# A scatter-add of whole rows of expert outputs, cut into two halves of 512 columns

## The reference

```python
D_MODEL = 1024; SEQ = 1024; N_EXPERTS = 16; TOP_K = 2; D_EXPERT = 256

def hier_moe(h, router_wg, router_bg, router_we, router_be, exp_w1, exp_w3, exp_w2):
    ...
    gate = jnp.sum(jax.nn.one_hot(expert_id, N_EXPERTS, dtype=jnp.float32) * top_w[..., None], axis=1)
    y = jnp.zeros((B * S, D), jnp.float32)
    for e in range(N_EXPERTS):
        hid = jax.nn.silu(xt @ exp_w1[e]) * (xt @ exp_w3[e])
        y = y + gate[:, e:e + 1] * (hid @ exp_w2[e]).astype(jnp.float32)
    return y.reshape(B, S, D).astype(h.dtype)

def trunk(x, ...):
    h = layer_norm(x, ln_in_g, ln_in_b)
    for l in range(DEPTH):
        mix = mixer(h, ...)          # attention and a gated linear recurrence, side by side
        h = layer_norm(DEEPNORM_ALPHA * h + mix, ln1_g[l], ln1_b[l])
        ffn = hier_moe(h, ...)
        h = layer_norm(DEEPNORM_ALPHA * h + ffn, ln2_g[l], ln2_b[l])
    return h
```

## Time and profile before

| | us |
|---|---|
| median of 3 runs | 1660.35 |
| lowest and highest of them | 1652.62, 1660.93 |
| the profiled execution | 1657.61 |
| its span (first to last instruction) | 1655.9 |
| its mean granted TensorE clock | 0.943 |

### The profile page before, as it was taken

One profiled execution on the slowest core, in us unless ns is written; L12 is line 12 of the kernel. 1 busy time (PEld: TensorE's weight loads), 2 busy tenths in 40 slices (PEclk: granted clock), 3 DMA queues, 4 the chain that ended last, 5 costly groups with the idle time before them and its releaser, 6 DMA issues. The chain is left out here.

```text
span 1655.9 us, 29919 instructions
## 1 busy us (share of the span) xinstructions
PE 1490.1 (90%) x9130; PEld 1307.0 (79%) x9131; DVE 1102.4 (67%) x2101; ACT 904.5 (55%) x1527; POOL 490.9 (30%) x345
## 2 busy tenths in 40 slices
PE   5999989999897999999999999985699999999940
PEld 5999967787687899999999999981577788777830
DVE  8788539999834877788877778877543433444237
ACT  3444447878734655655565566632465544555325
POOL 1221125665510011111112111121445444554318
PEclk9999999999956999999999999996899999999975
DMA  8865443444243212211111212116699777796566
GB/s 280 313 220 210 176 154 126 154 166 178 108 137 124 69 34 96 65 69 57 58 59 57 95 60 74 46 53 215 193 267 273 197 220 192 209 274 174 108 206 263
DMA packets 124005, 249.58 MB, mean 151 GB/s; under 512 B 22290, under 2 KB 75538, under 8 KB 123924
## 3 DMA queue, kind: packets, MB, share of 16 engines
q1 hardware_dynamic: 93984, 160.97, 28.0%
q0 software_dynamic: 12528, 45.62, 11.8%
q10 hardware_dynamic: 17412, 41.96, 6.6%
HBM read 153.98 MB, written 94.54 MB: 150 GB/s over the span
## 5 line engine op out<-in xcount | busy, mean ns | idle before, releaser
L1690 DVE TENSOR_TENSOR d_probs_t_lo<-d_pt_ps,d_probs_t_hi 128x512 fp32r<-128x512 f32 x256 | 164.6, 684 | 70.4 <-ACT d_probs_t_hi L1615 69.2
L1854 POOL TENSOR_TENSOR d_h_tile<-d_s_tile,d_ln_g_b 128x512 f32<-128x512 f32 x30 | 38.9, 1297 | 554.7 <-ACT d_s_tile L1636 536.1
L1615 ACT ACTIVATE d_probs_t_hi<-d_pt_ps 128x512 fp32r<-128x512 f32 x256 | 139.2, 595 | 110.3 <-PE d_pt_ps L1494 103.9
L1666 DVE TENSOR_REDUCE d_neg_max<-d_s_ps 128x1 f32<-128x1024 f32 x128 | 155.5, 1215 | 3.3 <-PE d_s_ps L1483 3.3
L121 PE MATMUL acc<-k_hi,wl_hi 128*128 128x256 f32 x512 | 144.6, 283 | 4.5 <-DVE k_lo L577 4.5
L1598 ACT ACTIVATE d_probs<-d_s_ps,d_neg_max 128x1024 f32<-128x1024 f32 x128 | 143.4, 1120 | 4.3 <-DVE d_neg_max L1666 4.3
L121 PE MATMUL e_a_ps<-up_hi,e_xt_hi 128*128 x336 | 137.1, 408 | 8.7 <-issue 4.4
L122 PE MATMUL acc<-k_lo,wl_hi 128*128 128x256 f32 x512 | 143.7, 281 | 0.0
L123 PE MATMUL acc<-k_hi,wl_lo 128*128 128x256 f32 x512 | 143.6, 280 | 0.0
L1512 PE MATMUL d_ot_ps<-d_probs_t_hi,d_v_split 128*128 128x256 f32 x512 | 127.5, 287 | 10.0 <-DVE d_probs_t_lo L1690 10.0
L1494 PE MATMUL d_pt_ps<-ident,d_probs 128*128 128x128 f32 x1024 | 133.7, 274 | 2.8 <-ACT d_probs L1598 2.8
(11 more groups left out here) (404 smaller groups left out, 4106.8 us busy)
## 6 DMA issues: line engine op xcount, KB each, us to landing
up_raw<-in_exp_w SPq DMA_DIRECT2D x32, 1024.0 KB, 10.3
down_raw<-in_exp_w SPq DMA_DIRECT2D x16, 1024.0 KB, 11.7
d_h_tile<-h_dram SPq DMA_DIRECT2D x16, 522.0 KB, 4.8
h_dram<-v_all ACTq DMA_DIRECT2D x16, 512.0 KB
ht_hi_dram<-k_hi ACTq DMA_DIRECT2D x8, 1024.0 KB, 4.3
ht_lo_dram<-k_lo ACTq DMA_DIRECT2D x8, 1024.0 KB, 6.7
q_dram<-wq_raw ACTq DMA_DIRECT2D x16, 512.0 KB, 2.9
d_q_tile<-q_dram SPq DMA_DIRECT2D x16, 512.0 KB, 3.9
```

The source lines that it names most:

```text
L1615: act.activation(pt_hi[:, c * HALF:(c + 1) * HALF, h % 2], pt_ps[c][:], ACT.Copy).then_inc(pth_done[c], 1)
L1666: dve.tensor_reduce(nm[:, u, h:h + 1], s_ps[h % 2][:], AX, ALU.max, negate=True).then_inc(nm_done, 1)
L1690: dve.tensor_tensor(pt_lo[:, part, h % 2], pt_ps[c][:], pt_hi[:, part, h % 2].bitcast(F32), ALU.subtract)\
```

## The change

The sums lie in two tensors of 512 columns each, `sum_dram[0]` and `sum_dram[1]`, instead of one of 1024. Each tile's scatter becomes two, one per half of the columns, each to its own tensor and with its own semaphore `y_added[c]`. The scatter of half c waits for ScalarE's half c of the tile and for the scatter of half c of the tile before. All stores and loads of the sums are cut in two in the same way, and the counts that are waited for follow.

```diff
-    sum_dram = nc.dram_tensor("sum_dram", (T + P, D), F32, kind="Internal").ap()
+    sum_dram = [nc.dram_tensor(f"sum_dram{c}", (T + P, D // 2), F32, kind="Internal").ap() for c in range(2)]
...
             def store_h1(t):
                 sp.wait_ge(h1_done, 2 * t + 2)
-                for dst in (h1_dram, sum_dram):
-                    sp.dma_start(dst[bass.ds(t * P, P), :], h1[:]).then_inc(h1_stored, 16)
-
-            sp.sem_inc(h1_stored, 32)
+                sp.dma_start(h1_dram[bass.ds(t * P, P), :], h1[:]).then_inc(h1_stored, 16)
+                for c in range(2):
+                    sp.dma_start(sum_dram[c][bass.ds(t * P, P), :], h1[:, c * 512:(c + 1) * 512]).then_inc(h1_stored, 16)
+
+            sp.sem_inc(h1_stored, 48)
...
             sp.wait_ge(last_h1, 2)
-            for dst in (h1_dram, sum_dram):
-                sp.dma_start(dst[T - P:T, :], s_t[1][:, 0:D]).then_inc(h1_stored, 16)
-            sp.wait_ge(h1_stored, 32 * NT + 64)
+            sp.dma_start(h1_dram[T - P:T, :], s_t[1][:, 0:D]).then_inc(h1_stored, 16)
+            for c in range(2):
+                sp.dma_start(sum_dram[c][T - P:T, :], s_t[1][:, c * 512:(c + 1) * 512]).then_inc(h1_stored, 16)
+            sp.wait_ge(h1_stored, 48 * NT + 96)
...
             last = sp.value_load(last_tile[0:1, 0:1], min_val=1, max_val=MT - 1)
-            sp.wait_ge(y_added, 16 * last + 16)
-            sp.nop(nofuse=True)
-            for t in range(EARLY):
-                sp.dma_start(first_rows[t], sum_dram[t * P:(t + 1) * P, :]).then_inc(rows_in[t], 16)
+            for c in range(2):
+                sp.wait_ge(y_added[c], 16 * last + 16)
+                sp.nop(nofuse=True)
+                for t in range(EARLY):
+                    sp.dma_start(first_rows[t][:, c * 512:(c + 1) * 512], sum_dram[c][t * P:(t + 1) * P, :]).then_inc(rows_in[t], 16)
...
             def down(j, u):
                 pool.wait_ge(gate_done, j + 1)
                 pool.nop(nofuse=True)
-                pool.wait_ge(yt_done[0], j + 2)
-                pool.nop(nofuse=True)
-                pool.wait_ge(yt_done[1], j + 2)
-                pool.nop(nofuse=True)
-                need(pool, y_added, 16 * j)
-                pool.nop(nofuse=True)
-                pool.indirect_dma_start(sum_dram, bass.IndirectOffsetOnAxis(sx[u][:, 0:1], 0), yt[u][:], None,
-                                        compute_op=ALU.add).then_inc(y_added, 16)
+                for c in range(2):
+                    pool.wait_ge(yt_done[c], j + 2)
+                    pool.nop(nofuse=True)
+                    need(pool, y_added[c], 16 * j)
+                    pool.nop(nofuse=True)
+                    pool.indirect_dma_start(sum_dram[c], bass.IndirectOffsetOnAxis(sx[u][:, 0:1], 0),
+                                            yt[u][:, c * 512:(c + 1) * 512], None, compute_op=ALU.add).then_inc(y_added[c], 16)
...
-                need(dve, y_added, 16 * (j - 1))
-                dve.nop(nofuse=True)
+                for c in range(2):
+                    need(dve, y_added[c], 16 * (j - 1))
+                    dve.nop(nofuse=True)
...
             for t in range(EARLY, NT):
-                sp.dma_start(x[t], sum_dram[t * P:(t + 1) * P, :]).then_inc(x_in[t], 16)
+                for c in range(2):
+                    sp.dma_start(x[t][:, c * 512:(c + 1) * 512], sum_dram[c][t * P:(t + 1) * P, :]).then_inc(x_in[t], 16)
```

More of the change, by code:

```diff
@@ L2215, in experts @@
         gate_done = sem("gate_ready")
-        y_added = sem("y_added")
+        y_added = [sem(f"y_added{c}") for c in range(2)]
         block = ctx.enter_context(nc.Block())
@@ L2348, in _ @@
             last = run_tiles(pool, skip, ahead, None, skip, skip, down, skip, split_rest)
-            pool.wait_ge(y_added, 16 * last + 16)
-            pool.nop(nofuse=True)
+            for c in range(2):
+                pool.wait_ge(y_added[c], 16 * last + 16)
+                pool.nop(nofuse=True)
             pool.wait_ge(x_in[1], 8 * last + 24)
```

10 lines of the change are left out of this document (5 added, 5 removed).

## The result

The changed kernel is slower: 1668.95 us (median of 6 runs, 1661.28 to 1676.55) against 1655.51 us (6 runs of the kernel before, 1651.55 to 1660.93). The ratio on record is 1.0069, 95% interval 1.004 to 1.0098, so 11.4 us (6.6 to 16.2); the quotient of the two medians, 1.0081 or 13.4 us, lies within that interval. The forecast was +0.2 us, and its range was 1652 to 1669 us. The profiled execution of the changed kernel took 1676.55 us with a span of 1674.8 us; it is the slowest of its six, so its trace shows the loss enlarged.

A forecast was written before the change was run, and what follows sets the result against it. TensorE's matmuls bound the expert stage, the scatter only the tail. Terms 0 + 0 + 0 + 0.2 = +0.2 us gave 1657.8 us against the profiled 1657.6, 1660.5 on the median's scale; range 1652 to 1669 us.

The forecast's parts named there:

- TensorE as busy as now: Sign of being right: in the expert loop, from 1200 to 1500 us, TensorE's busy share stays unchanged.
- its three signs of being wrong: TensorE's first matmul waiting for up_lo; DMA share near full in the loop; last stage's first load sooner with the stage.
- Part 1, GpSimd's order: Expert loop: second scatter makes GpSimd 1.89 us later, within up_lo's slack of 2.36 us at the tightest; price zero.
- Part 1, the last sentence: Expert loop: VectorE's added wait ahead of the gate copy is for a scatter already landed; zero.
- Part 2, the DMA engines: Expert loop: 2 KB packets and 1.0 us more start per tile raise DMA share to 88%; zero on TensorE.
- Part 3, the tail: After the last matmul: landing seen 0.9 us sooner, given back by SyncE's twelve issues; zero, -1.7 to +3.8 us.
- The third rival: Tail: the last landing, not SyncE's issues, sets the barrier; 0.9 us gained, up to 2.6; chance 12%.
- The halves don't land apart: Tail: the queue runs both halves as one, so SyncE's twelve issues start later; +2.8 us, 1663.3 us; chance 10%.
- Part 4, the last stage: Final layer norm: twenty loads behind the barrier, no engine waits for one; zero, bound 1.4 us.
- Part 5: Attention stage: one more store per tile, the last issued 0.4 us later; +0.2 us (0 to +0.5).
- The loop breaks: Expert loop: GpSimd's delay stalls TensorE at two-tile experts, from 3 us on; 15 us at 5 us, 1675 us; chance 8%.

The follow-up runs named there:

- the moved gate copy: VectorE's gate copy put behind the next tile's hidden rows: 0.9974 in the changed kernel, 0.9976 in the kernel before, both against the kernel before.
- ScalarE's loads above: Changed kernel with gate copy moved and weights signalled early, ScalarE instead of SyncE issuing the six early loads of half 1: 0.9947 to the kernel before.
- The runs with doses: Kernel before, whole scatters, a memset behind each making GpSimd 1.0, 3.5 or 4.8 us later: 1.0008, 1.0136 and 1.0206.
- the kernel with both repairs: Gate copy moved behind the hidden rows and weights signalled early: 0.9940 in the changed kernel, 0.9955 in the kernel before, both against the kernel before.
- the kernel with halved loads: Kernel before with one tensor and one scatter per tile, but stores and loads of the sums cut in two: 1.0024.
- the kernel with the memset of 1400 columns: Kernel before, one scatter per tile, with a GpSimd memset of 1400 columns behind each scatter that nothing waits for just then: 1.0008.
- the kernel with the small memset: Kernel before, one scatter per tile, with a GpSimd memset of 250 columns behind each scatter, awaited before going on: 1.0136.

## Where the prediction was right and where it was wrong, point by point

The measured median of 1668.95 us lies within the stated range, 0.05 us below its upper end. That is luck and no credit to the mechanism: the forecast was +0.2 us, the loss was 11.4, and the upper part of the range was there for a TensorE that waits for `up_lo`, which it didn't. Of its own signs of being right, "TensorE as busy as now" failed, with 94.2 us of 100 against 97.5; none of its three signs of being wrong clearly appeared. It looked for the loss on the wrong way.

**Part 1, GpSimd's order: the amount right, the price of zero wrong.** The issue of a half was put at 1.59 us and measures 1.58, the delay at 1.89 us and `up_lo` comes 2.1 to 2.2 us later. (The lower bound of 0.4 us leaves out one gap; two issues of 0.98 us with two gaps of 0.30 against 1.89 are 0.67 us. Nothing rests on it.) And, as forecast, TensorE never waits for up_lo on GpSimd. The step that failed is the list of those who wait for what is behind the scatter. It named TensorE as the only waiter for `up_lo` and `down_lo`, and measured the slack on that way alone: 3.09 us, 2.36 at the tightest. SyncE waits for the same `down_lo`, and its signal to ScalarE stands behind that wait. The trace of before has ScalarE waiting for the signal already, 11.9 us in 4 waits, so what makes `down_lo` later could make `up_hi` later. The runs put the price of this way at 3.6 us of the profiled loop.

**Part 1, the last sentence: "it is for the scatter of two tiles back, which has landed: zero".** This is the dearer error: the moved gate copy gives the changed kernel 1% of its time and the kernel before 0.24%, and the traces show 6.6 us in the four tiles and 4.7 us of lost clock behind three of them. The list of waits of the kernel before has this very wait, 3 times with 1.3 us in all, so it had not always landed. What moved it further: lateness adds up on GpSimd over a tile, from the two scatters over the weights and the gather to the next tile's second half, which started 3.3 us later than the whole one had; and VectorE has to see the later half landed. The half's shorter way makes up for 1.6 us of that: in the tail a whole scatter is seen landed 6.30 us after its start, a half after 1615.51 - 1610.77 = 4.74 us.

**Part 2, the DMA engines: right.** The 0.52 MB of scatter and as much of gather per tile took 45.6% x 360/38.66 = 4.25 us of DMA time per MB, and take 46.6% x 360/37.17 = 4.51, so some 0.3 us more per tile where 1.0 us was allowed for. The packets of 2 KB cost next to nothing. By the figures of the Trainium skill ("DMA: Bandwidth & Descriptors", section "Anatomy of one DMA"), 2.0 us plus the bytes at 436 GB/s, a half was, as an estimate, to land 0.6 us sooner than a whole. The trace disagrees: 6.30 - 4.74 = 1.56 us sooner in the tail (5.98 to 6.30 us in the seven profiles with whole scatters, 4.48 to 4.84 in the seven with halves), and the measurement decides. The transfer of 3.6 us that I read from the earlier trace rows for 0.52 MB, and the 2.3 us for half of it, fit that: 1.3 us.

**Part 3, the tail: the steps right, the end wrong by 1.3 us.** Against the end of ScalarE's last output (1589.15 before, 1609.34 after) the half scatters were to go out at 1.75 and 3.65 us, and went at 1.43 and 3.46; SyncE was to start at 6.55 us and end its twelve issues at 12.15, and did so at 6.17 and 12.20 (12.18 before). So the issues did give the landing back. But "the end of SyncE's issues opens the last stage" didn't hold for the kernel before: its barrier opened 14.66 us after the last output, 2.48 us behind the issues, and now it opens at 13.32, 1.12 us behind them. The third rival ("the barrier is set by the last landing") had the mechanism of before; its gain was 1.3 us, between the 0.9 and the 2.6 that it names, and the issues then took over as the limit. "The halves don't land apart" is refuted by SyncE's start 2.1 us ahead of half 1's earliest landing (1612.80 + 4.85 = 1617.65, with the 4.85 us from ScalarE's loads above).

**Part 4, the last stage: the price right.** From VectorE's first instruction behind the barrier to the end it takes 52.1 us before (1655.9 - 1603.81) and after (1674.8 - 1622.66). VectorE does wait 1.9 us for its first half tile, which the forecast had excluded; the stage's end doesn't show it.

**Part 5: not told apart.** The first expert tile starts anywhere from 1164.65 to 1173.40 us in the 14 profiles, with a mean of 1168.8 for two stores per tile and 1169.2 for three. 0.2 us can't be seen in that; nor do the 2.35 us of the first two profiles mean anything.

**The rivals.** "The loop breaks" was the right family, at 8%: GpSimd is late and TensorE stalls. But it decided from a delay of 3 us, because it had the same single waiter in view as part 1. The runs with doses put the knee near 1 us, and the slope at 8.5 to 9 us for each further us of lateness, that is 0.9 x 8.5 = 8 us for the 1.9 us that the forecast itself had, as an estimate from that line.

## What to carry to other kernels

Before an engine is made later for nothing, search the list of waits of the kernel before for every wait, on any engine, that ends with something it makes or something queued behind it: a wait of some tenths of a microsecond there, three times in 42, says that its waiter has no slack left, whatever the slack on the way that you had in view. It doesn't say what the lateness costs: here 1.0 us of it made the waits more (the gate copy's from 1.3 to 2.7 us, ScalarE's for the signal from 11.9 to 20.1 us) and the kernel 1.3 us longer, which can't be told from nothing, and the change's 2.1 us cost 11.4. A wait ahead of a tiny bookkeeping copy holds everything behind it on VectorE; put the copy behind the work that the critical engine needs, and give signals before waits that don't concern them. Once both were done here, the split cost nothing in the loop (396.5 and 396.6 us), and the kernel with both repairs is the best measured, with the split or without it: 0.994 (0.9916 to 0.9963) and 0.9955 (0.9939 to 0.9971), whose difference can't be told from nothing.

## What the runs showed of the hardware

**A short idle can cost TensorE half its clock for three more microseconds.** Behind the idle of the first chain's tile (12, the one behind tile 11), TensorE of the changed kernel (stretches of 1 us, columns as in the earlier trace rows):

```profile
1298.00:1299.00 1.00, 0.00 (x0) 0.00 (x0) 0.85 (x5) 0.04 (x1) 0.00 (x0) 1.00 0.00 0
1299.00:1300.00 1.00, 0.33 (x1) 0.34 (x2) 0.00 (x0) 0.96 (x1) 0.77 (x1) 0.90 0.00 0
1300.00:1301.00 1.00, 1.00 (x3) 0.73 (x3) 0.52 (x1) 1.00 (x2) 0.70 (x2) 0.50 0.21 25
1301.00:1302.00 1.00, 1.00 (x4) 0.79 (x3) 0.71 (x1) 0.04 (x1) 1.00 (x1) 0.50 0.56 143
1302.00:1303.00 1.00, 1.00 (x4) 0.81 (x3) 0.00 (x0) 0.00 (x0) 1.00 (x1) 0.50 0.86 352
```

The granted clock is 0.50, the level of 1.2 GHz, for three microseconds of full work after some two without a matmul, and the tile takes 11.07 us where its like take 9.5. In the kernel before, a place with almost as much idle (three slices busy for 0.32, 0.44 and 0.70) kept 1.00:

```profile
1416.00:1417.00 1.00, 0.32 (x2) 0.00 (x0) 1.00 (x3) 0.86 (x2) 0.00 (x0) 1.00 0.00 0
1417.00:1418.00 1.00, 0.44 (x2) 0.20 (x2) 1.00 (x3) 0.43 (x2) 0.00 (x0) 1.00 0.00 0
1418.00:1419.00 1.00, 0.70 (x3) 0.62 (x4) 0.76 (x5) 0.03 (x1) 0.00 (x0) 1.00 0.00 0
```

In the changed kernel's profile four tiles of 42 are lengthened so, by 1.5 to 2.6 us, 7 us of the 17.8 together; the kernel before has none. One of the four is the second tile of the stage, behind a stall that the kernel before has too; the other three, 4.7 us, stand behind waits of the first chain. In the kernel with halved loads the place that kept 1.00 above had 1.62 us of idle in three slices and not 1.54; there the clock fell to 0.50 and the tile behind took 11.06 us. So a stall of some 2 us cost 1.5 to 2.6 us more than itself, and not each time: the second tile of the stage is hit in 5 of the 9 profiles in which the first one has stalled TensorE.

**GpSimd's rows overlap.** What comes behind a scatter whose row is 1.6 us long starts while that row still lasts, mostly 1.0 to 1.2 us after it began (1.15 in the earlier trace rows, 1.02 in the kernel with the memset of 1400 columns), unless it is another scatter, which starts 1.88 us after it. And in the kernel with the small memset, the wait for it kept GpSimd idle for more than three times its length:

```profile
1245.63 0.90 POOL L2346 MEMSET e_idle<- 128x250 f32 x1
1249.48 2.41 POOL L2243 TENSOR_TENSOR up_lo<-up_raw,up_hi  x1 [2.95 <-issue]
```
